# Mean squares of the norms: six of eight squared chunks added on VectorE, three ones-multiplications in place of eight

## The chip, the cores and the metric

The kernel runs on one core of a Trainium2 chip. The metric is the device time of one execution in microseconds, as the median of several runs. In the text, PE is TensorE (PEld its weight loads), DVE is VectorE, ACT is ScalarE, POOL is GpSimd and SP is SyncE; a name with a q behind it (PEq, DVEq) is that engine's sequencer.

## What is computed

Two layers of a hybrid diffusion backbone over 384 tokens (128 context, 256 latent) with 1024 channels, all in fp32. Each layer norms its input twice:

```python
def rms_norm(x, g):
    xf = x.astype(F32)
    y = xf * lax.rsqrt(jnp.mean(xf * xf, axis=-1, keepdims=True) + EPS)
    return (y * g.astype(F32)).astype(x.dtype)

h = rms_norm(x, lw['norm1_g']) * (1 + sc1) + sh1
# projections of h, four mixers (recurrence, windowed attention, pooling, 2-D attention), merge
x = x + g1 * (merged @ lw['w_out'])
h2 = rms_norm(x, lw['norm2_g']) * (1 + sc2) + sh2
x = x + g2 * moe(h2, ...)      # router, 32 experts of which 4 for a token, a shared expert
```

The change touches only the sum over the channels of `xf * xf`. It is needed four times: before the first projection, between mixers and experts of layer 0, between the layers, and between mixers and experts of layer 1. Here these places are called site A, B, C and D, in that order.

## The kernel before, in words

Activations lie transposed: `xT` is 128 partitions x 8 chunks x 384 tokens, so a token's channels are spread over the partitions and over the chunks. A mean square is made in three steps. ACT squares each chunk (`squares` of the scalar block, L1353) into `sq`, which the profile calls `arena`. PE multiplies each squared chunk with a 128x128 matrix of ones (`mean_square`, recorded under the helper's line L787), all eight accumulating in one PSUM bank; this adds over partitions and chunks and leaves the sum on every partition. ACT takes the root (`root`, L1357), DVE the reciprocal (L1675) and the product with x and the scale (`norm`, L1682), ACT adds the shift (`shift`, L1364 and L1365), and only then can PE go on with the projection (A and C) or the router (B and D).

Every fp32 matmul is recorded as two passes (two MATMUL and two LDWEIGHTS), so the mean square is a row of x16.

The order on every engine is the order in which its block is written; semaphores join them. What stands around each site:

- **A**: `xT` arrives whole, ACT squares eight chunks in a row, DVE prepares the gate bounds of the recurrence (`lbw`, three small operations that wait for `params_in`; ACT's exponential on them comes behind its root). Behind the mean square PE has four rounds of `mod_block` (a 2 MB block of `w_mod` times the conditioning, L787 `ab<-slot,scT`) and `mod_turned` (`vb<-con,mod_rows`), with ACT's `mod_row` between the two.
- **B and D**: PE multiplies with `w_out` in eight groups, one for each chunk of x. DVE adds each to x (`residual`, two operations, L1956 and L1958), tells `x_ready`, ACT squares it. Behind the last group PE has the mean square, then `mod_block`s and `mod_turned`s, then the router. The first two matmuls of the mean square also release the two slots of `w_out` to SP's loads.
- **C**: PE adds the expert sums of each chunk by multiplying with the identity, four into the banks `vb` and four into `ab`; DVE's `residual` and ACT's squares follow. Then PE has one `mod_turned`, the mean square and two `mod_block`s.

DVE's helpers: `tell(s)` is a drain that increments `s`, `settle()` a drain, `empty` waits for a filled bank and frees it.

Of the kernel before, what the change touches and what calls it, by code (L numbers as in the profile page):

```python
# [6 lines left out]
ALU = mybir.AluOpType  # L7
ACT = mybir.ActivationFunctionType
# [4 lines left out]
KC = D // P  # L13
T = 384
# [100 lines left out]
LOOP_JOB = sum(units[0] < 2 * LOOP_PAIR for _, units in JOBS)  # L115
SHARED = T // HB
PIECE = 1024
TABLE_AFTER = 4
TABLE_BANK = (TABLE_AFTER - 1) % NBANK

# [129 lines left out]
def build(nc, A, O):  # L250
    ctx = ExitStack()
    with ctx:
        def sb(name, shape):
            return ctx.enter_context(nc.sbuf_tensor(name, shape, F32))

        def sem(name):
            return ctx.enter_context(nc.semaphore(name))

        slots = [sb(f"slot{i}", [P, SLOT]) for i in range(NSLOT)]
        xT = sb("xT", [P, KC, T])  # L260
# [69 lines left out]
        def ar(*shape):  # L330
            n = 1
            for s in shape:
                n *= s
            a = arena[:, used[0]:used[0] + n]
            used[0] += n
            assert used[0] <= 11520, used[0]
            if len(shape) == 2:
                return a.rearrange("p (a b) -> p a b", b=shape[1])
            if len(shape) == 3:
                return a.rearrange("p (a b c) -> p a b c", b=shape[1], c=shape[2])  # L340
            return a
# [36 lines left out]
        sq = ar(KC, T)  # L378
# [41 lines left out]
        def c_(name):  # L420
            return con[:, CN[name][0]:CN[name][1]]
# [23 lines left out]
        c_loaded = sem("c_loaded")  # L445
        x_ready = sem("x_ready")
        sq_ready = sem("sq_ready")
        h_ready = sem("h_ready")
        root_wanted = sem("root_wanted")
        root_ready = sem("root_ready")  # L450
# [103 lines left out]
        def _(sp):  # L554
# [15 lines left out]
            for l in range(DEPTH):  # L570
# [68 lines left out]
                def in_pieces(x):  # L639
                    return x.rearrange("p (i w) -> p i w", w=PIECE)  # L640

# [139 lines left out]
        def _(pe):  # L781
# [3 lines left out]
            def mm(out, lhsT, rhs, start, stop, last=False):  # L785

                i = nc.tensor.matmul(out, lhsT, rhs, start=start, stop=stop, skip_group_check=True)  # L787
                if release and not last:
                    i.then_inc(release.pop(0), 1)
                return i  # L790

            def group(ring, body):

                b = ring.next()
                banks, full, free = (vb, vfull, vfree) if ring is v else (ab, afull, afree)
                pe.wait_ge(free[b], 1).then_inc(free[b], -1)  # L796
                last = body(banks[b])
                last.then_inc(full[b], 1)
# [24 lines left out]

            def mean_square():
                def squares(o):
                    for c in range(KC):
                        pe.wait_ge(sq_ready, 1).then_inc(sq_ready, -1)
                        last = mm(o[:, 0:T], c_("ones"), sq[:, c, :], c == 0, c == KC - 1, c == KC - 1)
                    return last
                group(a, squares)  # L830

            def wview(w, c=KC):
# [36 lines left out]
            for l in range(DEPTH):  # L869
# [60 lines left out]
                for r in range(2):  # L930
# [15 lines left out]
                    for t in ((0, 1, 2), (0, 2, 1))[r]:  # L946
                        pe.wait_ge(vx_ready, 1).then_inc(vx_ready, -1)
                        banks = pair_of_banks()
                        for pr in range(2):
                            for rt in range(2):  # L950
                                rows = slice(64 * rt, 64 * rt + 64)
                                for h2 in range(2):
                                    h = 2 * pr + h2
                                    last = mm(vb[banks[rt]][64 * h2:64 * h2 + 64, 256 * pr:256 * pr + 256],
                                              kdN[rows, t, 64 * h:64 * h + 64], VX[rows, h, 0:256], True, True, True)
# [4 lines left out]
                    for t in range(NT):  # L960
                        banks = pair_of_banks()
                        for pr in range(2):
                            for h2 in range(2):
                                last = mm(vb[banks[h2]][:, P * pr:P * pr + P], KE[64 * h2:64 * h2 + 64, pr, P * t:P * t + P],
                                          QE[64 * h2:64 * h2 + 64, pr, P * t:P * t + P], True, True, True)
                                if pr == 1:
                                    last.then_inc(vfull[banks[h2]], 1)
                    for t in range(NT):
# [7 lines left out]
                        for pr in range(2):  # L976
                            for g in range(4):
                                row = TC * t + 2 * g + (t > 0) + r
                                for h2 in range(2):
                                    q = slice(64 * h2, 64 * h2 + 64)  # L980
                                    last = mm(vb[banks[h2]][32 * g:32 * g + 32, P * pr:P * pr + P],
                                              QX[q, pr, P * t + 32 * g:P * t + 32 * g + 32],
                                              S[q, pr, row:row + 2, :].rearrange("p a b -> p (a b)"), False, True, True)
# [167 lines left out]
                o = vb[3]  # L1151
# [30 lines left out]
                for n in range(SHARED):  # L1182
                    if n == TABLE_AFTER:
                        pe.wait_ge(entries_ready, 1).then_inc(entries_ready, -1)
# [109 lines left out]
                for c, (ring, b) in enumerate(sums):  # L1294
                    bank, full = (vb[b], vfull[b]) if ring is v else (ab[b], afull[b])
                    for t in range(NT):
                        if c == 0:
                            pe.wait_ge(acc_added, 1).then_inc(acc_added, -1)
                        last = mm(bank[:, P * t:P * t + P], acc[:, t, c:D:KC], ident, False, t == NT - 1)
# [6 lines left out]
        def _(act):  # L1306
            a = Cursor(range(NBANK))
            f = nc.scalar.activation
# [24 lines left out]
            for l in range(DEPTH):  # L1333
# [16 lines left out]
                def squares():  # L1350
                    for c in range(KC):
                        act.wait_ge(x_ready, 1).then_inc(x_ready, -1)
                        f(sq[:, c, :], xT[:, c, :], ACT.Square).then_inc(sq_ready, 1)  # L1353

                def root():

# [10 lines left out]
                def mod_row(rows=mod_rows[:, :]):  # L1367
                    empty(lambda o: f(rows, o[:, :], ACT.Copy))
                    tell(mod_rows_ready)

                squares()
                root()
                if l == 0:
# [139 lines left out]
                for u in range(UNITS):  # L1513
                    gates(PASSES[1], u)
                warm(ACT.Sqrt)
                squares()
                root()
                warm(ACT.Sigmoid)
# [20 lines left out]
                def silus(b):  # L1539
                    act.wait_ge(hid_full[b], 1).then_inc(hid_full[b], -1)  # L1540
                    return f(si[b], vb[b][:, 0:P], ACT.Silu)  # L1541
# [11 lines left out]
                for n in range(SHARED + 1):  # L1553
# [5 lines left out]
                    elif n < SHARED:  # L1559
                        silus(b).then_inc(si_ready, 1)  # L1560
                    if n == TABLE_AFTER:
                        a.next()
# [42 lines left out]
        def _(dve):  # L1605
            v = Cursor(range(NBANK))
            vec = nc.vector

            def settle():

                dve.drain()

            def tell(s):
                dve.drain().then_inc(s, 1)  # L1614
# [17 lines left out]
            dve.drain().then_inc(x_ready, KC)  # L1632
            for l in range(DEPTH):
                v.restart()
                dve.wait_ge(params_in, 32 if l == 0 else 16).then_inc(params_in, -32 if l == 0 else -16)

                if l == 0:
# [83 lines left out]
                for r in range(2):  # L1721
# [41 lines left out]
                    for t in ((0, 1, 2), (0, 2, 1))[r]:  # L1763
# [5 lines left out]
                        for c in order:  # L1769
                            row = TC * t + c + (t > 0)  # L1770
                            for pr in range(2):
                                b = b0 if c < TC // 2 else b1
                                at = 256 * pr + HD * (c % (TC // 2))
                                last = vec.scalar_tensor_tensor(
                                    S[:, pr, row + 1 - r, :], S[:, pr, row + r, :],
                                    tot[:, NCH * pr + TC * t + c:NCH * pr + TC * t + c + 1],
                                    vb[b][:, at:at + HD], ALU.mult, ALU.add)
# [171 lines left out]
                tell(merged_ready)  # L1949
                scales(1)  # L1950

                def residual(s, take=empty):

                    for c in range(KC):
                        def add(o):
                            vec.scalar_tensor_tensor(xT[:, c, 0:P], o[:, 0:P], mT[:, l, s, c, 0:1], xT[:, c, 0:P],  # L1956
                                                     ALU.mult, ALU.add)
                            return vec.scalar_tensor_tensor(xT[:, c, P:T], o[:, P:T], mT[:, l, s, c, 1:2], xT[:, c, P:T],  # L1958
                                                            ALU.mult, ALU.add)
                        take(add)  # L1960
                        tell(x_ready)

                residual(2)
                inverse_root()
# [115 lines left out]
                for t in range(NT):  # L2080
                    k = slice(TOPK * t, TOPK * t + TOPK)
# [41 lines left out]
                for n in range(SHARED // 2, SHARED):  # L2123
                    if n == TABLE_AFTER:
                        unit_indices()
# [40 lines left out]
                    dve.wait_ge(afull[b], 1).then_inc(afull[b], -1)  # L2166
                    add(ab[b]).then_inc(afree[b], 1)

                residual(5, take_sum)
                if l == 0:  # L2170
                    modulated(*TAIL_MODS[1])
            tell(y_ready)
# [135 lines left out]
```

## Time and profile before

| what | value |
|---|---|
| time, median of 3 runs | 1756.45 us (1753.31 to 1760.62) |
| span of the profiled execution | 1753.3 us |
| PE busy | 1610.8 us (92%) |
| DVE busy | 519.8 us (30%) |
| ACT busy | 409.7 us (23%) |
| mean granted clock of PE | 0.968 of full speed |
| mean DMA rate | 220 GB/s |

The profiled execution's span lies at the low end of the runs: it is 3.15 us under their median. PE busy counts the modelled length of each matmul; a waiting engine does not count as busy. The time of a site is read in the rows of its stretch, from the last chunk of x to the first matmul that needs the normed input.

### The profile page before, as it was taken

Reading aid. Unit: us, or ns where it says so; the run is one execution under the profiler, and the core shown is the slowest. Engines: PE = TensorE matmul, PEld = TensorE weight load, DVE = VectorE, ACT = ScalarE, POOL = GpSimd, SP = SyncE. Lnnn points to the kernel's source line nnn. Section 1 sums busy time; section 2 is a strip of 40 time slices with the busy share of each in tenths; the row PEclk is TensorE's granted clock in tenths of the full one; section 3 lists DMA queues with packets and bytes.
Section 4 is the critical chain, followed back from the end, with each engine's and each line's share of the span. In section 5 each row is a group of like instructions: output and inputs, shape, how many; then the busy total and the mean of one; then the engine's idle time right before and its main releaser. Section 6 shows DMA issues by size and latency. Waiting matters only on the chain. (4 is left out here: it accounts for less than half of the span.)

```text
span 1753.3 us, 26420 instructions
## 1 busy us (share of the span) xinstructions
PE 1610.8 (92%) x9104; PEld 1016.1 (58%) x9104; DVE 519.8 (30%) x1311; ACT 409.7 (23%) x895; POOL 219.1 (12%) x182
## 2 busy tenths in 40 slices
PE   6999989999999988898889999899999999888897
PEld 2666656655686554455466656566558655555555
DVE  2055754411124111111141557542111431111113
ACT  2233324510122111111132332443001311111110
POOL 0003200000001132232100022000000022232320
PEclk7999999999998999999999999999999899999999
DMA  9512244552426999999993024416132299999994
GB/s 349 218 60 91 46 150 162 172 173 97 144 95 268 337 378 392 367 362 392 341 337 110 25 96 100 148 54 204 51 142 96 101 354 366 389 368 358 384 378 145
DMA packets 166114, 385.84 MB, mean 220 GB/s; under 512 B 21020, under 2 KB 58908, under 8 KB 165536
## 3 DMA queue, kind: packets, MB, share of 16 engines
q1 hardware_dynamic: 140976, 340.28, 52.6%
q0 software_dynamic: 16992, 24.96, 5.9%
q10 hardware_dynamic: 8016, 18.90, 3.0%
q8 instruction: 77, 1.26, 0.3%
q14 instruction: 53, 0.43, 0.1%
HBM read 372.27 MB, written 31.98 MB: 231 GB/s over the span
## 5 line engine op out<-in xcount | busy, mean ns | idle before, releaser
L787 PE MATMUL ab<-hT,slot 128*128 128x384 f32 x1344 | 451.5, 491 | 11.2 <-PEq L815 6.2
L787 PEld LDWEIGHTS ab<-hT,slot 128*128 128x128 f32 x1344 | 255.6, 192 | 194.0 <-issue 25.1
L787 PE MATMUL vb<-slot,arena 128*64 128x256 f32 x2560 | 307.9, 395 | 61.2 <-PEq L837 61.1
L787 PEld LDWEIGHTS vb<-slot,arena 128*64 128x64 f32 x2560 | 206.2, 142 | 145.8 <-issue 80.6
L689 POOL DMA_INDIRECT expert_sums<-arena,sum_index x72 | 112.9, 1568 | 362.2 <-POOLq L678 177.0
L2100 DVE SCALAR_TENSOR_TENSOR arena<-vb,unit_gate,arena 128x128 f32<-128x128 f32 x80 | 28.0, 350 | 381.4 <-DVEq L2099 381.4
L787 PE MATMUL ab<-slot,hT 128*128 128x384 f32 (+1 forms) x384 | 118.1, 463 | 0.0
L1541 ACT ACTIVATE arena<-vb 128x128 f32<-128x128 f32 x92 | 25.5, 277 | 362.6 <-ACTq L1540 362.6
L787 PE MATMUL vb<-nat,arena 128*64 128x512 f32 (+1 forms) x480 | 107.8, 532 | 1.8 <-PEq L935 1.1
L821 PEld LDWEIGHTS ab<-con,arena 128*128 128x128 f32 x532 | 60.1, 145 | 80.2 <-issue 79.0
L787 PE MATMUL vb<-yT,slot 128*128 128x384 f32 x288 | 103.0, 486 | 0.0
L1414 ACT ACTIVATE con<-ab,sm 128x384 f32<-128x384 f32 x64 | 37.2, 582 | 277.5 <-ACTq L1312 277.3
L1838 DVE TENSOR_TENSOR con<-vb,con 128x384 f32<-128x384 f32 x48 | 26.8, 559 | 234.4 <-DVEq L1618 234.4
L787 PEld LDWEIGHTS ab<-slot,hT 128*128 128x128 f32 x384 | 71.7, 190 | 41.9 <-issue 4.6
L821 PE MATMUL ab<-con,arena 128*128 128x128 f32 x532 | 85.7, 291 | 10.4 <-PEq L796 10.4
L787 PE MATMUL vb<-arena 64*32 64x128 f32 (+4 forms) x920 | 77.3, 360 | 14.8 <-PEq L1052 10.5
L787 PE MATMUL vb<-merged,slot 128*128 128x384 f32 x256 | 85.0, 495 | 4.2 <-PEq L796 4.2
L2106 DVE COPY arena<-vb 128x512 f32<-128x512 f32 x80 | 55.3, 691 | 112.6 <-DVEq L2105 112.6
L734 POOL TENSOR_TENSOR arena<-arena 128x128 f32<-128x128 f32 x6 | 3.7, 616 | 662.1 <-POOLq L733 662.1
L787 PEld LDWEIGHTS vb<-merged,slot 128*128 128x128 f32 x256 | 80.2, 314 | 9.2 <-issue 6.8
L1548 ACT ACTIVATE arena<-ab 128x512 f32<-128x512 f32 x80 | 47.3, 597 | 151.4 <-ACTq L1312 151.4
L787 PEld LDWEIGHTS vb<-yT,slot 128*128 128x128 f32 x288 | 54.7, 190 | 38.1
(270 smaller groups left out, 1501.7 us busy)
## 6 DMA issues: line engine op xcount, KB each, us to landing
slot<-in_w_up SPq DMA_DIRECT2D x64, 2048.0 KB
slot<-in_w_mod SPq DMA_DIRECT2D x24, 2048.0 KB
slot<-in_w_mgate SPq DMA_DIRECT2D x32, 1024.0 KB
nat<-in_w_down SPq DMA_DIRECT2D x32, 1024.0 KB, 18.0
slot<-in_w_in SPq DMA_DIRECT2D x10, 2048.0 KB
arena<-in_w_down SPq DMA_DIRECT2D x16, 1024.0 KB
hT<-in_w_down SPq DMA_DIRECT2D x16, 1024.0 KB, 20.3
slot<-in_w_out SPq DMA_DIRECT2D x4, 2048.0 KB
```

Of the source, the lines that this page charges most:

```text
L689: pool.indirect_dma_start(sum_d[b], bass.IndirectOffsetOnAxis(ap=index.bitcast(U32), axis=0), Y[b], None, bounds_check=2 * T - 1, oob_is_e ...
L734: nc.gpsimd.tensor_tensor(aa[n % 2], si[n % 2], ups[n % 2], ALU.mult)
L787: i = nc.tensor.matmul(out, lhsT, rhs, start=start, stop=stop, skip_group_check=True)
L821: last = nc.tensor.transpose(bank[:, P * k:P * k + P], x, ident)
L1414: empty(lambda o: f(gb[u % 2], o[:, 0:T], ACT.Sigmoid, bias=s_("bmg")[:, col:col + 1]))
L1541: return f(si[b], vb[b][:, 0:P], ACT.Silu)
L1548: empty(lambda o: f(XT[b][:, 4 * g:4 * g + 4, :], o[:, :].rearrange("p (a b) -> p a b", b=P), ACT.Copy))
L1838: empty(lambda o: vec.tensor_tensor(g, o[:, 0:T], g, ALU.mult))
L2100: vec.scalar_tensor_tensor(aa[b], vb[b][:, P:2 * P], g, si[b], ALU.mult, ALU.mult)\
L2106: vec.tensor_copy(dst, vb[2 + b][:, :]).then_inc(vfree[2 + b], 1)
```

## The change

DVE adds the squares of chunks 0 to 5 into `sq[:, 0, :]`, one addition at a time, each followed by a drain. PE multiplies chunk 6, chunk 7 and that sum with the ones, in this order. In `residual` the additions lie behind the residuals of chunks 3 to 7 (the k-th addition behind chunk k + 2); at site A all five run in a row, ahead of the small operations on `lbw`. ACT's squares of chunks 6 and 7 are told on a semaphore of their own.

```diff
+SUMMED = KC - 2
...
             def mean_square():
                 def squares(o):
-                    for c in range(KC):
-                        pe.wait_ge(sq_ready, 1).then_inc(sq_ready, -1)
-                        last = mm(o[:, 0:T], c_("ones"), sq[:, c, :], c == 0, c == KC - 1, c == KC - 1)
-                    return last
+                    for c in range(SUMMED, KC):
+                        pe.wait_ge(late_sq_ready, 1).then_inc(late_sq_ready, -1)
+                        mm(o[:, 0:T], c_("ones"), sq[:, c, :], c == SUMMED, False)
+                    pe.wait_ge(sq_sum_ready, 1).then_inc(sq_sum_ready, -1)
+                    return mm(o[:, 0:T], c_("ones"), sq[:, 0, :], False, True, True)
                 group(a, squares)
...
-                        f(sq[:, c, :], xT[:, c, :], ACT.Square).then_inc(sq_ready, 1)
+                        f(sq[:, c, :], xT[:, c, :], ACT.Square).then_inc(sq_ready if c < SUMMED else late_sq_ready, 1)
...
+                def sum_squares(k):
+
+                    dve.wait_ge(sq_ready, 2 if k == 1 else 1).then_inc(sq_ready, -2 if k == 1 else -1)
+                    vec.tensor_tensor(sq[:, 0, :], sq[:, 0, :], sq[:, k, :], ALU.add)
+                    tell(sq_sum_ready) if k == SUMMED - 1 else settle()
+
+                if l == 0:
+                    for k in range(1, SUMMED):
+                        sum_squares(k)
                 dve.wait_ge(params_in, 32 if l == 0 else 16).then_inc(params_in, -32 if l == 0 else -16)
...
-                def residual(s, take=empty):
+                def residual(s, take=empty, squared=True):
...
                         tell(x_ready)
+                        if squared and c > KC - SUMMED:
+                            sum_squares(c + SUMMED - KC)
...
-                residual(5, take_sum)
+                residual(5, take_sum, squared=l == 0)
```

On PE at site C, between the `mod_turned` ahead of the mean square and the `mod_block` behind it (and in the same way at B and D), the rows were:

```order
L787 MATMUL ab<-arena,con 128x384 [waits afree0,sq_ready]
L787 MATMUL ab<-arena,con 128x384 [waits sq_ready] x7
```

and are now:

```order
L790 MATMUL ab<-arena,con 128x384 [waits afree0,last_two_squares_ready]
L790 MATMUL ab<-arena,con 128x384 [waits last_two_squares_ready]
L790 MATMUL ab<-arena,con 128x384 [waits squares_of_the_first_six_chunks_summed]
```

Five matmuls are gone; the first one now waits for the square of chunk 6, where it waited for chunk 0.

On DVE at site C, the residuals of chunks 4 to 7 (the filled banks `afull2` to `afull1`) stood back to back:

```order
L1956 SCALAR_TENSOR_TENSOR xT<-ab,mT,xT 128x128 [waits afull2]
L1958 SCALAR_TENSOR_TENSOR xT<-ab,mT,xT 128x256
L1956 SCALAR_TENSOR_TENSOR xT<-ab,mT,xT 128x128 [waits afull3]
L1958 SCALAR_TENSOR_TENSOR xT<-ab,mT,xT 128x256
L1956 SCALAR_TENSOR_TENSOR xT<-ab,mT,xT 128x128 [waits afull0]
L1958 SCALAR_TENSOR_TENSOR xT<-ab,mT,xT 128x256
L1956 SCALAR_TENSOR_TENSOR xT<-ab,mT,xT 128x128 [waits afull1]
L1958 SCALAR_TENSOR_TENSOR xT<-ab,mT,xT 128x256
```

and the same stretch with the additions, from the one behind chunk 3 on:

```order
L1643 TENSOR_TENSOR arena<-arena 128x384 [waits sq_ready]
L1970 SCALAR_TENSOR_TENSOR xT<-ab,mT,xT 128x128 [waits afull2]
L1972 SCALAR_TENSOR_TENSOR xT<-ab,mT,xT 128x256
L1643 TENSOR_TENSOR arena<-arena 128x384 [waits sq_ready]
L1970 SCALAR_TENSOR_TENSOR xT<-ab,mT,xT 128x128 [waits afull3]
L1972 SCALAR_TENSOR_TENSOR xT<-ab,mT,xT 128x256
L1643 TENSOR_TENSOR arena<-arena 128x384 [waits sq_ready]
L1970 SCALAR_TENSOR_TENSOR xT<-ab,mT,xT 128x128 [waits afull0]
L1972 SCALAR_TENSOR_TENSOR xT<-ab,mT,xT 128x256
L1643 TENSOR_TENSOR arena<-arena 128x384 [waits sq_ready]
L1970 SCALAR_TENSOR_TENSOR xT<-ab,mT,xT 128x128 [waits afull1]
L1972 SCALAR_TENSOR_TENSOR xT<-ab,mT,xT 128x256
```

An addition now lies between each two residuals from chunk 3 on, and a fifth behind that of chunk 7.

## Rows read from the trace of the kernel before

**Rows 1.** The page's first part: busy time and share of the span.

```profile
PE 1610.8 (92%) x9104; PEld 1016.1 (58%) x9104; DVE 519.8 (30%) x1311; ACT 409.7 (23%) x895; POOL 219.1 (12%) x182
```

**Rows 2.** Timeline at B: start, length, operation, [idle before it, releaser].

```profile
512.41 5.32 PE L787 MATMUL ab<-arena,con 128*128 128x384 f32 x16
512.73 0.35 DVE L1956 SCALAR_TENSOR_TENSOR xT<-vb,mT,xT 128x128 f32<-128x128 f32 x1 [4.42 <-DVEq L1618]
513.00 0.47 DVE L1958 SCALAR_TENSOR_TENSOR xT<-vb,mT,xT 128x256 f32<-128x256 f32 x1
513.64 0.52 ACT L1353 ACTIVATE arena<-xT 128x384 f32<-128x384 f32 x1 [4.36 <-ACTq L1352]
...
517.67 3.64 PE L787 MATMUL ab<-slot,scT 128*32 128x512 f32 x32
...
522.26 0.40 ACT L1364 ACTIVATE hT<-hT,mT 128x128 f32<-128x128 f32 x1 [0.20 <-ACTq L1363]
```

**Rows 3.** Timeline at D.

```profile
1370.46 0.52 ACT L1353 ACTIVATE arena<-xT 128x384 f32<-128x384 f32 x1 [4.64 <-ACTq L1352]
...
1374.49 3.64 PE L787 MATMUL ab<-slot,scT 128*32 128x512 f32 x32
```

**Rows 4.** Timeline at C.

```profile
889.73 0.35 DVE L1956 SCALAR_TENSOR_TENSOR xT<-ab,mT,xT 128x128 f32<-128x128 f32 x1 [0.69 <-DVEq L2166]
...
894.02 0.35 DVE L1956 SCALAR_TENSOR_TENSOR xT<-ab,mT,xT 128x128 f32<-128x128 f32 x1 [0.69 <-DVEq L2166]
...
894.93 0.52 ACT L1353 ACTIVATE arena<-xT 128x384 f32<-128x384 f32 x1 [0.91 <-ACTq L1352]
...
899.86 3.64 PE L787 MATMUL ab<-slot,scT 128*32 128x512 f32 x32
...
910.32 14.86 PE L787 MATMUL ab<-hT,slot 128*128 128x384 f32 x40 [4.71 <-PEq L815]
```

**Rows 5.** Timeline at A.

```profile
9.77 3.42 ACT L1353 ACTIVATE arena<-xT 128x384 f32<-128x384 f32 x8 [5.05 <-ACTq L1352]
...
10.44 8.20 PE L787 MATMUL ab<-arena,con 128*128 128x384 f32 x16 [10.44 <-PEq L827]
...
11.85 0.34 PEld L787 LDWEIGHTS ab<-arena,con 128*128 128x128 f32 x1 [0.30 <-issue]
...
18.57 1.92 PE L787 MATMUL ab<-slot,scT 128*32 128x512 f32 x16
...
24.93 3.64 PE L787 MATMUL ab<-slot,scT 128*32 128x512 f32 x16
...
45.99 14.26 PE L787 MATMUL ab<-hT,slot 128*128 128x384 f32 x37 [1.52 <-PEq L815]
```

**Rows 6.** Windows: stretch and length, five engines busy, clock, DMA share, GB/s.

```profile
1.50:18.50 17.00, 8.06 (x16) 4.34 (x16) 0.58 (x4) 4.91 (x10) 0.00 (x0) 1.00 0.96 352
18.50:36.00 17.50, 12.81 (x65) 5.18 (x64) 7.87 (x23) 5.04 (x7) 0.00 (x0) 0.63 1.04 376
...
528.90:541.20 12.30, 10.30 (x64) 9.33 (x65) 4.48 (x29) 4.32 (x8) 0.00 (x0) 0.74 0.01 5
```

**Rows 7.** Timeline ahead of B, the first two groups of `w_out`.

```profile
469.01 0.56 DVE L1838 TENSOR_TENSOR con<-vb,con 128x384 f32<-128x384 f32 x1 [5.24 <-DVEq L1618]
469.66 0.56 DVE L1840 TENSOR_TENSOR merged<-merged,con 128x384 f32<-128x384 f32 x1
...
470.93 41.64 PE L787 MATMUL vb<-merged,slot 128*128 128x384 f32 x128 [2.08 <-PEq L796]
476.62 0.35 DVE L1956 SCALAR_TENSOR_TENSOR xT<-vb,mT,xT 128x128 f32<-128x128 f32 x1 [5.97 <-DVEq L1618]
...
481.77 0.35 DVE L1956 SCALAR_TENSOR_TENSOR xT<-vb,mT,xT 128x128 f32<-128x128 f32 x1 [4.41 <-DVEq L1618]
```

**Rows 8.** Windows of 1 us behind D: PE busy, granted clock, DMA share, GB/s.

```profile
1389.00:1390.00 1.00, 0.00 (x0) 1.00 0.00 0
...
1392.00:1393.00 1.00, 1.00 (x8) 0.50 0.00 0
```

More of the change, by code:

```diff
@@ L447, in build @@
         sq_ready = sem("sq_ready")
+        late_sq_ready = sem("last_two_squares_ready")
+        sq_sum_ready = sem("squares_of_the_first_six_chunks_summed")
         h_ready = sem("h_ready")
```

## The prediction, made before the changed kernel ran

> **What bounds the kernel now.** The page comes first: PE is busy 92% of the span [rows 1], so either PE's own work or a chain that PE waits for must shrink. That share says nothing of one stage, so I read the timeline at the four sites, and in each asked two things: what ended last before the root could be taken, and whether what lies behind is hung on the root or on something else.
>
> At B the squares of chunks 0 to 6 are long there when PE comes to them. PE starts its 16 passes at 512.41, DVE's last residual starts at 512.73, ACT squares it at 513.64 and is through at 514.16; the next work of PE starts at 517.67 [rows 2]. So the mean square is bound by PE: 5.26 us for 16 passes, 0.33 each, and the last square, which looks as if it set the end, lies under the first six passes or so. D is the same, with the last square at 1370.46 and the next work at 1374.49 [rows 3]. At C the last square ends at 894.93 + 0.52 = 895.45 and PE goes on at 899.86 [rows 4]: bound by PE again. At A ACT has all eight squares in 3.42 us from 9.77, PE needs 8.20 from 10.44 [rows 5]: bound by PE, at about half speed (a weight load of 0.34 and a gap of 0.30, so 0.64 for a pass).
>
> Behind the mean square: at B the first shift of the normed input begins at 522.26, 4.6 us behind the last pass, after root, reciprocal and the rows of two mod blocks [rows 2]; all of these hang on the end of the mean square, since PE's mod blocks stand behind it. At C PE waits 4.71 us for the normed input before the projection at 910.32 [rows 4], a pure chain. Behind B the DMA engines are at a share of 0.01 from 528.9 to 541.2 [rows 6]: the expert loads wait for the ranking, and so move with the router. Nothing there runs ahead by the clock on the wall, so what a site gives should reach the end of the span.
>
> **The change, part by part.** Three prices are needed first.
>
> An addition of 128x384 out of and into SBUF: L1840 has this shape and takes 0.56; it starts at 469.66, 0.09 behind the end of L1838 (469.57), with a drain between [rows 7]. So 0.65 for an addition with its drain. From ACT's square to PE's pass: the first square of A ends at 9.77 + 0.52 = 10.29 and PE starts at 10.44 [rows 5, 2], 0.15. A PE that starts from idle: the first group of `w_out` starts at 470.93 and its residual at 476.62, 5.69 later; the groups follow each 5.15 (481.77 - 476.62), and in the full flow a residual starts 0.32 behind a group's end (512.73 - 512.41) [rows 7, 2]. So 5.69 - 0.32 - 5.15 = 0.22 is the price of starting from idle. Not every wait need cost it: bounds 0 and 0.22, I take 0.22.
>
> *B.* PE does chunk 6 at 512.41 and is idle from 513.07. Chunk 7: square ends 514.16, + 0.15 + 0.22, then four passes (chunk 7 and the sum) of 0.33: 515.85. Is the sum there in time? The residual of chunk 7 ends at 513.47, the fifth addition runs from 513.56 to 514.12; PE asks for it at 515.2. It is 1 us early. The end moves from 517.67 to 515.85: **1.8 us**. Five matmuls are 3.3 us, of which 1.5 go back into a wait for DVE and ACT that they used to cover. The other four additions cost nothing, for DVE is idle 4.42 us ahead of each residual [rows 2]; without that cover each would be 0.65.
>
> *D.* The square ends at 1370.98, so the end is 1370.98 + 0.15 + 0.22 + 1.32 = 1372.67 in place of 1374.49: **1.8 us** [rows 3].
>
> *C.* Here DVE has little room. From 889.73 to 894.02 are three residuals, 1.43 each, of which 0.69 is waiting [rows 4]; the work is 0.74 (512.73 to 513.47 [rows 2]). With an addition a turn is 0.74 + 0.09 + 0.56 + 0.09 = 1.48, so DVE becomes the slower one by 0.05 a turn, for the four additions ahead of chunk 7: 0.2. Chunk 7's square then ends at 895.45 + 0.2 = 895.65, and PE ends at 895.65 + 0.15 + 0.22 + 4 x 0.34 = 897.38, in place of 899.86: **2.5 us**. If the wait between drain and addition costs as much as the way from DVE to ACT (513.47 to 513.64, 0.17) on both sides, a turn is 1.64, the delay 4 x 0.21 = 0.84 and the gain 1.8. I take 2.5, since L1838 and L1840 are the nearest row.
>
> For this addition there is another price in the Trainium skill. "VectorE: DVE Perf Modes", in the section on the errata of SBUF sources, gives 58 cycles and one for each element, which is 0.46 us for 384 at 0.96 GHz, as an estimate. By it the turn would be 1.38, C would lose nothing, and the sum would be 0.2 better. The row with its 0.56 disagrees, and it decides.
>
> *A.* Chunk 6's square ends at 9.77 + 6 x 0.414 + 0.52 = 12.77 (0.414 is (3.42 - 0.52) / 7), PE starts at 12.77 + 0.15 + 0.22 = 13.14. Six passes of 0.64 end at 16.98; before, 16 passes took 8.20 and not 10.24, so the last ones ran at full speed from about 16, and if that holds again the end is near 16.6. In place of 18.57: 1.6 to 2.0, I take **1.7 us**. The five additions (first at about 10.8, 0.65 each) are through at 14.0, before PE asks for them (15.7). The three small operations on `lbw` come later by them, but before ACT's root is done. Does it reach the projection at 45.99? The rounds from 18.57 on (24.93 is the second block) are a chain of block, ACT, turned block. The loads do not hold them: until 18.5 some 17 x 352 = 6.0 MB came in [rows 6], of which some 1.9 MB are x and parameters and the rest two blocks of 2.1 MB but for 0.1; the other two are in by 18.5 + 4.3 / 0.376 = 30, and the fourth block will be wanted at 36.
>
> *Releases.* At B and D the slots of `w_out` go free with the mean square's first two matmuls. The second of these is now chunk 7, some 1.5 us later. At B SP's next load then is the shared expert's, which queues behind a 2 MB block of `w_mod`, over 5 us at the rates of [rows 6]; it costs nothing.
>
> Sum: 1.7 + 1.8 + 2.5 + 1.8 = 7.8 us. The profiled execution would go from 1753.3 to 1745.5; it lay 3.15 under the median, so the median goes from 1756.45 to 1748.6, which is 0.44% less. What a measurement of this kernel can tell from no change is about 0.5%, 8.8 us: the forecast is a real gain just under it.
>
> **The rivals.**
> 1. *Part of it is given back.* At A the mod blocks could after all wait for loads (gain 0), and at C DVE could need 1.64 a turn (1.8). Then 0 + 1.8 + 1.8 + 1.8 = 5.4: 1751. Against it: the megabytes above leave 4 us and more of room.
> 2. *The clock falls: slower than before.* PE now stands idle 1.2 us in the middle of B and D, right ahead of the narrow mod blocks. Behind D there is a stretch in which PE did nothing from 1389 to 1390 and the granted clock was 0.50 by 1392 [rows 8], 1.2 in place of 2.4 GHz. If the gap does that, four passes take 2.56 in place of 1.32 and two mod blocks 7.28 in place of 3.64 (one is 3.64 at half and 1.92 at full clock [rows 5]), so each of B and D loses 4.9 and gains 1.8: 3.1 worse. C loses 1.2 of its 2.5. Sum: -1.7 + 3.1 - 1.3 + 3.1 = +3.2, 1760; with folds and router at half clock too, up to 1766. It decides as soon as both B and D fall. Against it: in the rows behind D the gap lies between matmuls of 32 columns, at B and D behind 40 us of full ones. The Trainium skill, in "TensorE: Matmul & The Clock Gate", in the section on HAM oscillation, has idle stretches between bursts of matmuls send the clock to half; that is this rival.
> 3. *The mean square does not set the root*, and nothing moves: 1756. At B the mod rows and the norm come to the shift together [rows 2], but both hang on PE's end. Very unlikely.
> 4. *More than the sum*: no 0.22 at four starts and full clock at A give 9 us, 1747.
>
> **How the numbers follow.** The sum as it stands 0.62, part given back 0.17, the clock 0.10 (one site 0.05, both 0.05), nothing 0.05, more 0.06. The predicted time is the first's, 1748.6. Bounds of its prices are 1747 to 1750.3, and a median of a few runs moves by 3 us to both sides (the three runs lie 7 us apart), hence 1744; to the other side the range takes in part and nothing given, 1757.5. Faster by over 0.5% takes 8.8 us, a matter of 1 us above the sum: 0.28, mostly from the first case with an error in my favour. Within 0.5%: 0.66. Slower by over 0.5% only by the clock at both sites or worse: 0.06.
>
> **What would show it.** In the profile after: a mean square of x6 at every site; at B and D a wait of 1 to 1.4 us of PE ahead of chunk 7, and the mod blocks 1.8 us sooner behind the last residual (4.9 us after the start of the last residual before, 3.1 now); at C residuals 1.48 apart from chunk 4 on, and 3.2 us from the last residual's start to the mod blocks in place of 5.8; at A the first mod block at 16.6 to 17.0, the projection at 44.3. Wrong would be a granted clock of 0.50 on the mod blocks of B and D, a projection at A still at 46, or residuals of C more than 1.6 apart.

## The result, and the profile after

The changed kernel takes 1752.41 us (median of 20 runs, 1749.19 to 1757.26), the kernel before beside it 1757.03 (20 runs, 1752.6 to 1763.06): a ratio of 0.9974, 95% interval 0.9966 to 0.9983. That is 4.6 us less, where 7.8 were forecast. The span of the profiled execution is 1748.0 us. One execution of the kernel before in the last batch below took 2431.76 us at a granted clock of 0.65; the ratios leave it out.

The page's first part and the timeline at A, after:

```profile
PE 1595.0 (91%) x9064; PEld 1003.5 (57%) x9064; DVE 530.1 (30%) x1331; ACT 409.6 (23%) x895; POOL 218.8 (13%) x182
```

```profile
10.86 0.56 DVE L1643 TENSOR_TENSOR arena<-arena 128x384 f32<-128x384 f32 x1 [9.18 <-DVEq L1642]
11.61 0.56 DVE L1643 TENSOR_TENSOR arena<-arena 128x384 f32<-128x384 f32 x1 [0.19 <-ACT arena L1357]
...
12.93 4.18 PE L790 MATMUL ab<-arena,con 128*128 128x384 f32 x6 [12.93 <-PEq L830]
...
13.85 0.56 DVE L1643 TENSOR_TENSOR arena<-arena 128x384 f32<-128x384 f32 x1 [0.19 <-DVEq L1642]
...
17.04 2.83 PE L790 MATMUL ab<-slot,scT 128*32 128x512 f32 x16
...
41.85 1.62 PE L790 MATMUL ab<-hT,slot 128*128 128x384 f32 x2 [1.52 <-PEq L818]
```

Forty matmul records are gone (9104 in [rows 1]) and twenty additions have come. At A the first mod block starts at 17.04 in place of 18.57 [rows 5], the projection at 41.85 in place of 45.99.

The timeline at B, after:

```profile
508.67 0.81 PE L790 MATMUL ab<-arena,con 128*128 128x384 f32 x2
508.98 0.35 DVE L1970 SCALAR_TENSOR_TENSOR xT<-vb,mT,xT 128x128 f32<-128x128 f32 x1 [3.61 <-DVEq L1622]
...
509.57 0.55 SPq L565 DMA_DIRECT2D slot<-in_w_mod  x1
509.89 0.52 ACT L1357 ACTIVATE arena<-xT 128x384 f32<-128x384 f32 x1 [4.36 <-ACTq L1356]
509.97 0.56 DVE L1643 TENSOR_TENSOR arena<-arena 128x384 f32<-128x384 f32 x1 [0.25 <-DVEq L1642]
...
510.56 1.53 PE L790 MATMUL ab<-arena,con 128*128 128x384 f32 x4 [1.08 <-PEq L830]
...
512.02 3.64 PE L790 MATMUL ab<-slot,scT 128*32 128x512 f32 x32
...
519.27 1.92 PE L790 MATMUL ab<-slot,scT 128*32 128x512 f32 x16 [2.63 <-PEq L799]
```

From the last residual to the mod blocks it is 512.02 - 508.98 = 3.04 us, in place of 4.94 [rows 2]. But the third mod block has a wait of 2.63 us ahead of it. In this profile of the kernel before it followed the turned rows at once; its load had been issued by SP 0.59 us behind the start of the last residual:

```profile
513.32 0.55 SPq L562 DMA_DIRECT2D slot<-in_w_mod  x1
```

```profile
521.24 1.05 PE L787 MATMUL vb<-con,mod_rows 128*128 128x2 f32 x8
522.25 1.93 PE L787 MATMUL ab<-slot,scT 128*32 128x512 f32 x16
```

In the changed kernel too it is issued 0.59 us behind the last residual. The load hangs on the first matmul of the mean square, which follows the last group of `w_out` at once in both kernels; the block hangs on the end of the mean square; and only the second has moved. The bank that the block writes is no reason to wait: ACT's last eviction of a mod block ends at 516.41.

The timelines at D and C, after:

```profile
1364.93 0.35 DVE L1970 SCALAR_TENSOR_TENSOR xT<-vb,mT,xT 128x128 f32<-128x128 f32 x1 [3.61 <-DVEq L1622]
...
1366.51 1.53 PE L790 MATMUL ab<-arena,con 128*128 128x384 f32 x4 [1.08 <-PEq L830]
...
1367.96 3.64 PE L790 MATMUL ab<-slot,scT 128*32 128x512 f32 x32
```

```profile
889.39 0.35 DVE L1970 SCALAR_TENSOR_TENSOR xT<-ab,mT,xT 128x128 f32<-128x128 f32 x1 [0.19 <-DVEq L2182]
...
889.66 0.47 DVE L1972 SCALAR_TENSOR_TENSOR xT<-ab,mT,xT 128x256 f32<-128x256 f32 x1
...
890.38 0.56 DVE L1643 TENSOR_TENSOR arena<-arena 128x384 f32<-128x384 f32 x1 [0.25 <-DVEq L1642]
...
890.97 0.88 PE L790 MATMUL ab<-arena,con 128*128 128x384 f32 x2 [0.45 <-PEq L830]
891.13 0.35 DVE L1970 SCALAR_TENSOR_TENSOR xT<-ab,mT,xT 128x128 f32<-128x128 f32 x1 [0.19 <-DVEq L2182]
...
892.71 2.88 PE L790 MATMUL ab<-arena,con 128*128 128x384 f32 x4 [0.85 <-PEq L830]
...
895.52 3.92 PE L790 MATMUL ab<-slot,scT 128*32 128x512 f32 x32
```

At D the mod blocks come 3.03 us behind the last residual, in place of 4.94. At C, DVE's turn is 891.13 - 889.39 = 1.74 us (0.35 to 0.47 of work twice, an addition of 0.56, and waits of 0.25 ahead of it and 0.19 behind it); the last four passes take 2.88 us and not 1.4, for the granted clock falls as they start, behind a gap of 0.85 us (windows of 1 us: length, PE busy, granted clock, DMA share, GB/s):

```profile
892.00:893.00 1.00, 0.29 (x1) 0.86 1.06 389
893.00:894.00 1.00, 1.00 (x2) 0.50 1.05 385
```

From the first of the eight residuals to the mod blocks C takes 15.63 us, against 15.84 before.

### The profile page after: what moved, and what is told of

Its sections match the earlier page's. It is cut to its first block and busy times, and to the rows that moved or that the text cites. A ratio compares the mean times of both kernels' runs of the same rounds, so it can differ in the third digit from the quotient of the medians.

```text
span 1748.0 us, 26380 instructions
## 1 busy us (share of the span) xinstructions
PE 1595.0 (91%) x9064; PEld 1003.5 (57%) x9064; DVE 530.1 (30%) x1331; ACT 409.6 (23%) x895; POOL 218.8 (13%) x182
## 5 line engine op out<-in xcount | busy, mean ns | idle before, releaser
L790 PE MATMUL ab<-hT,slot 128*128 128x384 f32 x1344 | 452.2, 492 | 10.1 <-PEq L818 5.9
```

## The experiments

Each kernel was timed beside the kernel before on the same chip. At B two steps are read: from the start of the last residual to the mod blocks, and from there to ACT's eviction of the router. "C" is from the first of the eight residuals to the mod blocks. The number in brackets behind a ratio is its 95% interval.

**C alone** (the other sites with eight multiplications), and **C alone with its additions on GpSimd**, in that engine's block where it is otherwise idle:

```diff
+SUMMED = ((0, 0), (6, 0))     # chunks added, by layer and norm
...
+if l == 0:                    # GpSimd's block, behind routed_done; not in residual()
+    for k in range(1, SUMMED[1][0]):
+        pool.wait_ge(sq_ready, 2 if k == 1 else 1).then_inc(sq_ready, -2 if k == 1 else -1)
+        nc.gpsimd.tensor_tensor(sq[:, 0, :], sq[:, 0, :], sq[:, k, :], ALU.add)
+        pool.drain().then_inc(sq_sum_ready, 1) if k == SUMMED[1][0] - 1 else pool.drain()
```

> The change at site C alone (between the layers); A, B and D multiply all eight squared chunks as before. Theory 1, the additions make VectorE's turn 1.74 us instead of 1.43 because each waits on a semaphore behind a drain: the last residual comes 1.2 us later against the start of the sums, and the site gives 1.2 us (time 0.07% less) where the clock stays full. Theory 2, TensorE's waits there (0.45 and 0.85 us between narrow work) let the granted clock fall to half: the last four passes take 2.9 us instead of 1.3 and the site gives 0 to 0.2 us. Rival, the site gives the forecast 2.5 us and the loss is elsewhere: time 0.14% less.

> As only_c, but the five additions of site C run on GpSimd, which is idle there, and VectorE's residuals stay as before. If VectorE's turn is a cause (theory 1), the residuals are 1.43 us apart again, the last square comes 1.2 us sooner than in only_c and the mean square ends some 2.5 us sooner than before the change; GpSimd's additions must then take under 1.43 us each. If the clock is a cause by itself (theory 2), the last four passes still take 2.9 us in this profile, although VectorE is free of the additions. If neither, no difference from only_c.

Measured: 1757.57 us, 0.9997 (0.9981 to 1.0014), and 1754.0 us, 0.9986 (0.9967 to 1.0004); the kernel before 1758.06. Alone, neither total can be told from no change. The timelines can be told apart. On VectorE the last residual is 11.24 us behind the first and C takes 15.65 us; on GpSimd it is 10.00 and C takes 13.03:

```profile
895.36 1.00 POOL L785 TENSOR_TENSOR arena<-arena 128x384 f32<-128x384 f32 x1 [0.25 <-ACT arena L1366]
896.60 1.00 POOL L785 TENSOR_TENSOR arena<-arena 128x384 f32<-128x384 f32 x1 [0.24 <-POOLq L784]
```

```profile
897.17 0.89 PE L796 MATMUL ab<-arena,con 128*128 128x384 f32 x2
898.25 1.53 PE L796 MATMUL ab<-arena,con 128*128 128x384 f32 x4 [0.19 <-PEq L836]
```

A GpSimd addition takes 1.00 us, nearly twice VectorE's 0.56, but it is out of the residuals' way. So VectorE's turn of 1.74 delays the end of C by 1.24 us in the changed kernel. The rest of the 2.62 between the two profiles is mostly the clock, which fell in the first and held in the second.

**A, B and D alone** (C as before), and **four chunks summed** at B, C and D (A stays at six):

```diff
+SUMMED = ((6, 6), (0, 6))     # the first kernel
+SUMMED = ((6, 4), (4, 4))     # the second
```

> The change at A, B and D, with C as before (eight multiplications, no additions there). If C gave next to nothing in the changed kernel, this one is as fast as the changed kernel (0.26% under before); by the forecast's own sum without C it would be 5.3 us, 0.30%, and 2.5 us slower than the full change should have been. If the gain of a site is swallowed by the load stream of the expert stages (rival), it is clearly under 0.2%.

> At B, C and D only four chunks are added by VectorE (three additions, behind the residuals of chunks 5 to 7) and TensorE multiplies five times; A stays at six. TensorE then works from the end of its last group to the last square nearly without a gap. Theory 1: at C two additions ahead of the last residual instead of four, 0.6 us late instead of 1.25. Theory 2: no idle ahead of the last matmuls, so the clock stays full there. Both: C gives about 1.9 us, B and D 1.9 each as before, the whole 6.5 to 7 us, 0.37 to 0.40% under before. If only the count of multiplications matters, it is slower than the changed kernel by two matmuls at three sites, 4 us.

Measured: 1751.62 us, 0.9971 (0.9950 to 0.9992), and 1752.91 us, 0.9969 (0.9949 to 0.9989). The totals only suggest that most of the gain is not C's. With four summed, C took 13.90 us: the last residual 10.62 behind the first, 0.62 late as its first theory had it, no gap ahead of the last matmuls, and the clock at 1.00. That is one profile. Both profiles have the wait ahead of B's third mod block, 2.85 and 2.92 us, and behind it the clock is at half: to the eviction B takes 15.25 and 14.90 us in place of 11.31. Neither expectation had that, and the next kernel was made for it.

**The first slot of `w_out` released earlier**, in layer 0: inside the last group, by the matmul behind its last reader, and not by the mean square. The edit moves a second thing too: the second slot is now released by the mean square's first matmul, so the shared expert's load is issued 0.59 us behind the last residual, in place of 2.55; no run takes the two moves apart. Then the same **with C on GpSimd** as well.

```diff
+def pairs_of(c):
+    for k in range(KC):
+        if c == KC - 1 and k == 4 and l == 0:
+            release.append(freed[wo[0][0]])
+        yield wview(wo[k // 4][1], 4)[:, k % 4, c:D:KC], merged[:, k, :]
...
-release.extend([freed[wo[0][0]], freed[wo[1][0]]])
+release.extend([freed[wo[0][0]], freed[wo[1][0]]] if l > 0 else [freed[wo[1][0]]])
```

> The changed kernel with one edit: in layer 0 the first w_out slot is released inside the last w_out group, by the matmul behind its last reader, instead of by the first matmul of the mean square. Nothing is left out. Theory (B's third mod block waits for its load, which is issued at the mean square and so moves with it): the load is issued about 3 us earlier against the last residual, the idle time of 2.6 us ahead of the third mod block (519.27 in the changed kernel) is gone, the step from the second site's mod blocks to the router's eviction is 11.3 us in place of 11.74, and the granted clock stays at 1.00 through it; in the median 0.4 us when the clock had stayed up and 3 to 4 us when it had fallen, so a ratio of 0.994 to 0.997 against the kernel before. Rival (the load is slow because the rest of the DMA traffic is, whenever it is issued): the block starts at the same time after the last residual, 10.3 us, and the ratio is that of the changed kernel, 0.9974. Second rival (loads ahead of it in the queue): as the first.

> The changed kernel with two edits: the five additions of the site between the layers stand in GpSimd's block instead of VectorE's, and the first w_out slot of layer 0 is released inside the last w_out group. Nothing is left out. Theory (the four sites are worth 1.5, 1.9, 2.8 and 1.9 us once VectorE's turn at the third is back at 1.43 and the load of the second no longer ends late): 8.1 us, ratio 0.9954; from the last residual to the mod blocks 3.04 us at the second and fourth site, and 13.0 us for the residuals of the third with what follows; granted clock 1.00 at all of them. Rival (what is won ahead of the expert stages is lost in them, since their loads and clock do not move with it): the sites show the same steps, but the ratio stays at that of the changed kernel, 0.997.

> The changed kernel as it was, beside the others on the same chip. If the clock's fall at the third site belongs to the gaps that the change opens there, the last four passes of its mean square take 2.9 us again and the granted clock is 0.50 a few us behind the last residual; if it was chance (the unchanged form fell in one profile of four), they take 1.3 us in most. The idle time ahead of the third mod block is again 2.6 to 2.9 us. Ratio 0.997 to 0.998 by both.

> The change at the third site alone once more, one profile, to read the clock there a second time. If the fall belongs to the two idle stretches of PE (0.45 and 0.85 us) between the turned mod rows and the last chunk: granted clock 0.50 and 2.9 us for the last four passes again, 15.6 us from the first residual to the mod blocks. If by chance: clock 1.00, 1.4 us, and 14.1 us in place of 15.84 of before.

Measured, the kernel before at 1758.14: early release 1750.13 us, 0.9960 (0.9943 to 0.9978); with C on GpSimd 1746.92 us, 0.9932 (0.9914 to 0.9951); the changed kernel again 1753.56 us, 0.9975 (0.9962 to 0.9989). The totals of the early release and of the changed kernel overlap in their intervals, so that step is read from the profiles; the kernel with both edits lies clear, and gains a little more than its expected 0.9954. In the profile of the early release the load is issued 2.0 us ahead of the last residual (509.57 there), and the block follows with no wait; from the mod blocks to the eviction it is 11.31 us again:

```profile
507.58 0.55 SPq L565 DMA_DIRECT2D slot<-in_w_mod  x1
```

```profile
516.18 1.05 PE L790 MATMUL vb<-con,mod_rows 128*128 128x2 f32 x8
517.16 1.92 PE L790 MATMUL ab<-slot,scT 128*32 128x512 f32 x16
```

The changed kernel's second profile has the wait again, and now the clock falls. The timeline, and windows of 1 us (length, PE busy, granted clock, DMA share, GB/s):

```profile
514.45 1.05 PE L790 MATMUL vb<-con,mod_rows 128*128 128x2 f32 x8
518.48 3.12 PE L790 MATMUL ab<-slot,scT 128*32 128x512 f32 x16 [2.98 <-PEq L799]
521.52 1.87 PE L790 MATMUL vb<-con,uT 128*128 128x2 f32 x8
523.33 2.79 PE L790 MATMUL ab<-hT,wr 128*32 128x384 f32 x16
```

```profile
516.00:517.00 1.00, 0.00 (x0) 1.00 1.01 352
517.00:518.00 1.00, 0.00 (x0) 1.00 1.01 381
518.00:519.00 1.00, 0.52 (x8) 1.00 1.00 406
519.00:520.00 1.00, 1.00 (x12) 0.53 1.04 430
520.00:521.00 1.00, 1.00 (x8) 0.50 1.00 414
...
535.00:536.00 1.00, 1.00 (x7) 0.50 0.00 0
```

PE stands for 3 us, the granted clock goes from 1.00 (2.4 GHz) to 0.50 (1.2 GHz) a little behind it and is still there at 536. From the last residual to the first expert load it is 33.57 us, against 28.51 in the kernel before. The first rival of the early release (the load lands when it lands) would have the block start 10.3 us behind the last residual; it starts 7.59 behind it, so that rival falls. The rival of the last kernel (what is won is lost among the experts) falls too: 0.9932 lies clear of the changed kernel's 0.9975.

C alone, profiled again, had the clock fall at C again, later and for less: 14.94 us. In the changed kernel's second profile it fell there too, but PE was still busy when it did, 0.1 us ahead of the first gap.

**PE's gaps at C filled** (with the early release), twice, **C on GpSimd without the early release**, and **the kernel before again**:

```diff
 for c in range(SUMMED, KC):
+    if fill:                  # layer 1's first norm only
+        for _ in range(2 if c == SUMMED else 4):
+            mm(o[:, T:T + P], c_("ones"), c_("ones"), True, True, True)
     pe.wait_ge(late_sq_ready, 1).then_inc(late_sq_ready, -1)
```

> The changed kernel with the early release, and at the third site PE's two idle stretches filled: two matmuls of ones with ones (128 columns, into a part of the bank that nobody reads) ahead of chunk 6 and four ahead of chunk 7, where it had waited 0.45 and 0.86 us. Nothing is left out. Theory 1 (the gaps bring the clock down): granted clock 1.00 through the mean square of that site, its last four passes 1.4 us in place of 2.9, 14.1 us from the first residual to the mod blocks in place of 15.65, ratio 0.995. Theory 2 (the fall comes with something else in this stretch, such as the narrow matmuls of the turned mod rows ahead of it): 0.50 again, 15.6 us or a little more, ratio 0.996.

> The same kernel, a second profile, to read the clock of the third site again: 1.00 by theory 1, 0.50 by theory 2.

> The changed kernel with the five additions of the third site on GpSimd, and the release of the w_out slot as the changed kernel has it. Nothing is left out. If the two edits of the fastest kernel add up (early release 0.9960 against 0.9975 of the changed kernel, both together 0.9932), this one gives 0.9947: 2.8 us better than the changed kernel or more, of which 2.8 is the difference of the third site (13.0 against 15.65 us when the clock holds). If only the release mattered, 0.9975 again. At the second site 2.6 to 3 us of idle time ahead of the third mod block, with the clock at 0.50 behind it in most profiles.

> The kernel before, a second profile: whether its third site keeps the granted clock of 1.00 from the last residual to the mod blocks (15.84 us from the first residual to them), and whether its second site has no wait ahead of the third mod block and 11.31 us to the router's eviction, in another execution too. Both if the steps are the kernel's own and not those of one profile.

In the filled kernel something is left out, other than its expectation says: the fillers begin a new accumulation in the same bank between chunks 6 and 7, and chunk 6, as I read it, is missing from this one sum. The work at C is otherwise the same; layer 1's choice of experts may differ, so the total and the reading at D are taken with care; A and B lie ahead of it.

Measured, the kernel before at 1757.39: filled 1751.07 us, 0.9965 (0.9945 to 0.9985); a single run more, 1752.93; C on GpSimd alone 1751.45 us, 0.9968 (0.9949 to 0.9986); the kernel before, a single run, 1761.95. C on GpSimd alone was to take 0.9947 if the two edits add up and 0.9975 if only the release matters; its interval holds 0.9975 and its lower end is just above 0.9947, so the total points to less than the full sum. With the gaps filled the clock held at C in one profile (14.29 us) and fell in the other (15.61). The second profile of the kernel before answers both of its questions with no: ahead of B's third mod block it waits 0.80 us, though the step to the eviction is 11.31 again, and at C, where it has no gap, the clock fell this time:

```profile
896.00:897.00 1.00, 1.00 (x10) 1.00 1.04 385
897.00:898.00 1.00, 1.00 (x5) 0.69 1.06 391
898.00:899.00 1.00, 1.00 (x2) 0.50 1.03 379
```

```profile
897.15 7.10 PE L787 MATMUL ab<-arena,con 128*128 128x384 f32 x16
```

So one profile of each kernel was too few to read C from. All fourteen together, in us: A is the start of the projection; B and D run from the last residual to the first expert load; C as above.

| site | eight multiplications | as changed | with the variant |
|---|---|---|---|
| A | 43.0 to 46.7, mean 45.5 (5) | 39.8 to 44.3, mean 41.7 (9) | |
| B | 28.5 or 28.6 four times, 30.1; mean 28.8 | 27.0, 30.3, 33.4, 33.6, 33.7; mean 31.6 | early release: 26.2, 26.3, 28.2, 28.2; mean 27.2 |
| C | 15.84, 17.53, 17.53; mean 17.0 | 14.94, 15.63, 15.65, 15.66, 15.66; mean 15.5 | GpSimd: 13.03, 13.04, 14.30; mean 13.5 |
| D | 27.3 to 28.2, mean 27.8 (5) | 25.3 to 25.6, mean 25.4 (9) | |

(B counts the kernel with four chunks summed as changed, with 30.3; at C it took 13.90 and is in no mean, and neither are the two filled ones.) By these means the changed kernel gains 3.8 - 2.8 + 1.5 + 2.4 = 4.9 us; 4.6 (3.0 to 6.0) was measured. The early release adds 4.4, so 9.3 (measured 7.0, 3.9 to 10.0); GpSimd at C adds 2.0, so 6.9 alone (5.6, 2.5 to 9.0) and 11.3 with the early release (12.0, 8.6 to 15.1). The measured gains are (1 - ratio) times the kernel before's median. The sums stand on few profiles, but none falls outside its interval. They also leave out the stretches between the sites, which differ by more from one execution to the next: from A to B's last residual 466.0 to 470.0 us, from B's first expert load to C 342.8 to 346.5. In the mean the nine profiles with six chunks at A lose 0.9 and 1.0 us there against the other five, and win 0.9 behind D's first expert load. So the close agreement of some of these sums with the totals may be luck.

## Why the prediction came out as it did

The time, 1752.4, lies in the range, and "within 0.5%" was the likeliest sign. The forecast of 1748.6 was 3.8 us too good: 3.2 of it in the gain, 0.6 because the kernel before took 1757.03 beside it and not 1756.45. By its own steps:

- **"PE does chunk 6 ... 515.85 ... 1.8 us" at B, and the same at D: right.** The wait of PE ahead of chunk 7 is 1.08 at both (1.0 to 1.4 said), the mod blocks come 3.04 and 3.03 us behind the last residual (3.1 said), 1.9 us sooner. The price of starting from idle was about 0.14, not 0.22: chunk 7 starts at 510.56, four passes of 0.33 would end at 511.88, the mod block starts at 512.02. D kept it, and reached its first expert load 2.4 us sooner in the mean.
- **"Releases ... it costs nothing" at B: wrong, and the failing step.** I asked about the shared expert's load, behind the second slot, and not about the third mod block's, behind the first, whose release did not move at all. That was the trap: the release stood still and its user came 1.9 us sooner. The block wants its load 7.1 us behind the issue (519.27 - 2.63 = 516.64, from 509.57). Where the block waited by 0.4 us or more, in seven profiles, it started 9.7 to 10.1 us behind it. In the five profiles with eight multiplications it started 8.9 to 9.8 behind, with waits of 0 to 0.16 and once 0.80: the room had been nearly used up before. I had taken "over 5 us at the rates of [rows 6]" for 2 MB. The packets of the trace tell what that leaves out. In the changed kernel nothing moves for 1.3 us, the load's sixteen completion writes land between 6.9 and 9.1 us behind the issue, and the block starts 0.64 behind the last of them; by then 0.6 MB of the next load have moved. In the nine profiles with any wait the block starts 0.63 to 0.80 us behind the last write, so it is this load that it waited for. The wait alone costs 0.4 us, 11.74 to the router's eviction in place of 11.31 where the clock held. What costs is the clock behind it: the four profiles in which it fell reach the first expert load 30.3 to 33.7 us behind the last residual, the one in which it held 27.0.
- **Rival 2, the clock: the mechanism came, at another place.** It was to fall through the 1.2 us gap ahead of chunk 7 at B and D. In none of the eight profiles with that gap, at B or D, did it fall before the two mod blocks behind it were through. It fell in four of five at or just behind the 2.6 to 3.0 us of waiting at B, a wait that I had excluded, and in none of four as far as the third mod block once that wait was gone or down to 0.44 us. B as a whole is 2.8 us slower than before in the mean, not 1.8 faster. "Nothing there runs ahead by the clock on the wall" was the sentence that hid it: a load does.
- **"A turn is ... 1.48" at C: mis-sized.** It measured 1.74, beyond the bound of 1.64 too: 0.25 and not 0.09 lies ahead of an addition that follows a drain, 0.19 behind it. My nearest row, L1840 behind L1838 [rows 7], is an addition that waits for no other engine; that this is the difference is my reading, for no run takes the wait on ACT's semaphore away. So chunk 7's square came 1.24 us late and not 0.2. The 0.46 us for this addition that the prediction names beside its own 0.56 is the general row of the Trainium skill's "VectorE: DVE Perf Modes" (the section on the errata of SBUF sources); for an fp32 tensor_tensor the same section gives 151 cycles and one for each element, 0.56 us at 384 as an estimate, and the trace's 0.56 agrees. The gain was 2.5 by forecast; with the clock held on both sides it would be some 1.5 (15.84 against 14.29 of the filled kernel), with the clock down on both sides 1.9 (17.53 against 15.65), in the mean 1.5. Reading 15.84 against 15.63, 0.2, from one profile each compares a held clock with a fallen one.
- **A, "1.7 us": right at its place and too small behind it.** The mod block comes 1.5 us sooner, and the additions are through by 14.41. The loads hold nothing up; rival 1 was wrong in this, and right in that C's turn is longer than the sum had it, so that its 1751 is the nearest of the times given. But the projection came 3.8 us sooner in the mean. Two of the nine profiles had all three later blocks at half speed, and reached it at 44.3, some 1.9 sooner than the four of the other kind that had the same (45.6 to 46.7): about the 1.7 of the forecast. With six passes the second or third block of the rounds ran wholly or partly at full speed in seven profiles of nine, with eight multiplications in one of five; in [rows 5] the second takes 3.64, in the changed kernel's second profile 1.92, as the timeline below shows (start, length). I had priced the rounds behind as unchanged. So some 2 of the 3.8 us are the clock's, which the forecast did not have. Why it stays up longer there no run tells.

```profile
22.42 1.92 PE L790 MATMUL ab<-slot,scT 128*32 128x512 f32 x16
...
26.42 2.59 PE L790 MATMUL ab<-slot,scT 128*32 128x512 f32 x16
```

- **The sum.** 1.7 + 1.8 + 2.5 + 1.8 came out as about 3.8 - 2.8 + 1.5 + 2.4. Two sites gave more than forecast and two less, so the total lies nearer to the forecast than its terms do: that the time lies in the range is in part luck. Rivals 3 and 4 did not come: the mod blocks moved with the mean square at every site, and the changed kernel's 1752.4 is far from the 1747 of rival 4.

## What to carry to other kernels

When a change makes an engine reach a piece of work sooner, ask of that piece's load when it is issued and what that hangs on; where the release stands still and the user moves up, the load needs to have had that much room, counted from its issue to the start of its user in a trace, not from its bytes alone. An addition of 0.56 us is not free on an engine with 0.69 us of waiting in a turn when 0.25 of waiting comes ahead of it and 0.19 behind; an engine that is slower but idle can be the better place, and here the two repairs together brought a change from 0.9974 to 0.9932 of the time before. And read two or three profiles of each kernel before a difference of a microsecond or two at one place is believed.

## What the runs showed of the hardware

- A 2 MB load on SP's queue, with 2 MB and 1 MB issued behind it while the engines together moved 380 to 410 GB/s, had its first completion write 6.8 to 7.2 us behind its issue and its last one 8.2 to 9.5 behind, in fourteen profiles; a waiting PE went on 0.63 to 0.80 us later, 9.0 to 10.1 us behind the issue. The Trainium skill, in "DMA: Bandwidth & Descriptors", in the section on the anatomy of one DMA, gives for loads issued from GpSimd a fixed 2.0 us and 436 GB/s, which is 6.8 us as an estimate. By that the block, which asks at 7.1 us, would not have waited; the trace disagrees, for a load issued from SP. Whether a load with none behind it would be ready sooner no run shows.
- A wait of PE of 2.6 to 3.0 us, with only short matmuls of 2 columns ahead of it, went with a fall of the granted clock to 0.50 in four profiles of five; one of 1.08 us between full matmuls was followed by two mod blocks at 1.00 in all sixteen cases (eight profiles, B and D). The Trainium skill, in "TensorE: Matmul & The Clock Gate", in the section on HAM oscillation, says that idle stretches spent on DMA waits send the clock to half; the trace agrees for the load's wait, in four of five.
- At C the clock fell in nine of fourteen profiles: in five of five with the gaps of 0.45 and 0.85 us (in one of them ahead of the first gap), in three of seven without a gap over 0.19, and in one of two with the gaps filled. Whether the gaps make it likelier stays open; they are not its only cause.
- VectorE's addition of 128x384 takes 0.56 us, GpSimd's 1.00, with 0.25 of waiting between two of GpSimd's.
